# A new list scheduler for the mixers of a three-block transformer kernel, with new filler matmuls

## The chip, the cores and the metric

The kernel runs on one core of a Trainium2 chip. The metric is the device time of one launch in microseconds (us), median of three runs. Lower is better.

## What is computed

The input is 256 tokens of width 1024, float32. Three blocks are applied in turn. Each is: half a SwiGLU feed-forward (width 2816), a mixer, half a second feed-forward, all with residual sums and RMS norms. The first block ends with a final norm, and so does the last.

```python
x = x + 0.5 * swiglu(rms_norm(x, ffn1_norm), w_gate, w_up, w_down)
x = x + hybrid_mixer(rms_norm(x, mix_norm), ...)      # block 1
x = x + 0.5 * swiglu(rms_norm(x, ffn2_norm), ...)
```

The mixer of block 1 (stage 1, "mix1") adds two gated branches: a dilated attention over 4 heads in 3 groups, and RWKV-7, a recurrence per head over 16 heads, `S_t = S_(t-1) diag(w_t) + (S_(t-1) a_t) b_t^T + v_t k_t^T`, `y_t = S_t r_t`, with small decay, rate and gate networks ahead of it and a group norm behind it. The mixer of blocks 2 and 3 (stages 5 and 8, "mix2") has three attentions: a chunked one with a bias by distance (6 heads, kind a), one over keys that an index picks (5 heads, kind b), and one with a latent key and value (5 heads, kind c), and an output product.

## The kernel before, in words

Every product of float32 data with a weight is made of three matmuls (`mm3`, L1584 to L1586): data and weights are split into a high and a low part, and high x high, high x low and low x high are summed in one PSUM bank. Weights stream from HBM in chunks of up to 128 x 2048 numbers (1 MB) into three raw buffers. ScalarE (ACT) copies a chunk's high part (L2130) and VectorE (DVE) subtracts it for the low part (L2493). This is step `split`. The two buffers `whi`/`wlo` alternate.

The order of the whole program is made by the class `Order` before any instruction is written. It appends steps such as `("r_x", s, g, k)` to one list, `P.steps`. Each engine's program then walks this list (`run`) and writes its own part of each step. So all engines meet the steps in the same order, an engine takes its instructions one after the other, and only semaphores tie the engines together.

Stages run one after the other: 0 feed-forward, 1 mix1, 2 feed-forward, 3 norm, 4 feed-forward, 5 mix2, 6 and 7 feed-forward, 8 mix2, 9 feed-forward, 10 norm. Inside a mixer, `woven(steady, rest, *chains)` mixes Python generators. The steady one, `dense`, gives the weight products: `shift_mm` (streams k, v, r of RWKV, 256 columns), `proj` (gates, 512 columns), `up`, `wout`. The other chains give the small steps. The weaver keeps a clock for each engine, fed with the durations of the table `PACE`, and takes the first chain whose input is ready at PE's clock. After each dense step dense rests `rest` us.

RWKV has 8 groups g of two heads. Before, each group is one chain: `r_lora` (decay and rate), `r_tanh`, `r_norm`, `r_scan`, `r_nrm`, `r_exp`, `r_key`, `r_wide`, three `r_scaled`, `r_vb`, `r_ka`, `r_bonus`, `r_pairs`, `r_masks`, `r_dt`, `r_dm0`, `r_g0`; then five rounds k of `r_xz` (POOL clears a buffer), `r_x` (PE, 16 matmuls of 64x32, L1866), `r_xc` (DVE, L2820), `r_d` (PE, 32 matmuls, L1878 and L1885), `r_dd` (DVE, L2830 and L2835); then `r_w`, `r_rp`, `r_yp`, three rounds of `r_st` (DVE, L2855) and `r_s` (PE, L1942 and L1944), `r_ys`, `r_mean`, `r_sq`, `r_var`, `r_wide2`, `r_lg` with `r_turn2`, `r_fin`. At most two groups are in the front part and three in all, by the number of buffers (`Slots`).

`BLANKS` says where PE gets filler matmuls: `('up', 1, 0, 0, 0): 22` puts 22 matmuls of 256 columns on a constant (`still`, L1593) into a free bank ahead of that step. They compute nothing that is used. They come in PE's order like any matmul.

Of the kernel before, what the change touches and what calls it, by code (L numbers as in the profile page):

```python
# [94 lines left out]
def down_after(m):  # L95
# [10 lines left out]
    "split": (("act", 0.6), ("dve", 0.7)), "shift_mm": (("pe", 1.45),), "shift_copy": (("act", 0.6),),  # L106
    "shift_mix": (("dve", 1.5),), "r_lora": (("pe", 0.9),), "r_tanh": (("act", 1.7),), "r_norm": (("pe", 0.45),),
    "r_scan": (("dve", 0.45),), "r_exp": (("act", 1.3),), "r_nrm": (("dve", 0.2),), "r_key": (("dve", 0.9),),
    "r_wide": (("pe", 0.25),), "r_scaled": (("dve", 1.0),), "r_vb": (("pe", 0.45), ("act", 0.8)),
    "r_ka": (("pe", 0.45), ("act", 0.8)), "r_bonus": (("pe", 0.45), ("dve", 0.4)), "r_pairs": (("pe", 1.3),),  # L110
    "r_masks": (("dve", 1.4),), "r_dt": (("dve", 1.0),), "r_dm0": (("pe", 0.35), ("act", 0.4)), "r_g0": (("pe", 0.35), ("act", 0.4)),
    "r_x": (("pe", 0.35),), "r_xc": (("dve", 0.3),), "r_d": (("pe", 0.8),), "r_dd": (("dve", 0.6),),
    "r_w": (("pe", 0.6), ("act", 0.6)), "r_rp": (("pe", 0.6), ("dve", 0.95)), "r_yp": (("pe", 1.1),),
    "r_st": (("dve", 0.25),), "r_s": (("pe", 0.25),), "r_ys": (("act", 0.6),), "r_mean": (("pe", 0.45), ("dve", 0.4)),
    "r_sq": (("act", 0.4),), "r_var": (("pe", 0.45), ("dve", 0.2)), "r_wide2": (("dve", 0.4),), "r_lg": (("pe", 0.9),),
    "rope1": (("dve", 2.2),), "att_qk": (("pe", 0.5), ("act", 0.8)), "att_score": (("pe", 0.9), ("dve", 1.1)),
    "att_soft": (("dve", 0.2), ("act", 1.0)), "att_turn": (("pe", 0.4), ("act", 0.6)),
    "att_out": (("pe", 1.0), ("dve", 0.5)), "up": (("pe", 1.4),), "r_turn2": (("pe", 0.25),), "r_fin": (("dve", 1.3), ("act", 0.4), ("dve", 0.4)), "wout": (("pe", 1.4),),
    "turn_iq": (("pe", 0.45), ("act", 0.6)), "turn_ik": (("pe", 0.15), ("act", 0.4)), "ix_score": (("pe", 0.4), ("act", 0.55)),
    "ix_sum": (("pe", 2.5), ("act", 0.35)), "lat_turn": (("pe", 0.25), ("act", 0.9), ("dve", 0.5)),  # L120
    "latent_up": (("pe", 1.0), ("act", 0.45)), "turn_c": (("pe", 0.35), ("act", 0.6)), "u_score_c": (("pe", 0.25), ("dve", 0.4)),
    "u_score_b": (("pe", 0.6), ("dve", 0.4)), "u_score_a": (("pe", 0.6), ("dve", 0.4)), "u_soft": (("act", 0.45),),
    "u_turn": (("pe", 0.2), ("act", 0.35)), "u_out": (("pe", 0.35),), "turn_b": (("pe", 0.45), ("act", 0.6)),
    "turn_a": (("pe", 0.45), ("act", 0.6)), "turn_out": (("pe", 0.25), ("act", 0.4), ("dve", 0.4)), "wout2": (("pe", 1.4),),
    "in2_out": (("act", 0.6),), "lat_sq": (("act", 1.9),), "lat_scale": (("dve", 0.75), ("act", 1.1)), "bias8": (("act", 1.5),),
    "ix_rope": (("dve", 2.8),), "ix_diag": (("dve", 1.2),), "ix_top": (("dve", 1.5),), "krope": (("dve", 1.2),),
    "ix_mask": (("dve", 0.7),), "brope": (("dve", 1.9),), "qrope": (("dve", 1.4),), "u_norm": (("dve", 0.7),),
    "proj": (("pe", 0.7),), "proj_out": (("dve", 0.7), ("act", 0.6)),
}
HOP = 0.25  # L130

BLANKS = {
    ('turn_x', 1, 0, 0): 6, ('proj', 1, 'qkv', 1, 0): 5, ('proj', 1, 'gate', 0, 0): 14,
    ('proj', 1, 'gate', 0, 4): 2, ('att_turn', 1, 0, 1, 0): 4, ('att_out', 1, 0, 0): 4, ('up', 1, 0, 0, 0): 22,
    ('r_wide', 1, 0): 3, ('r_wide', 1, 1): 3, ('shift_mm', 1, ('k', 1), 0, 4): 6, ('r_bonus', 1, 0): 10,
    ('r_d', 1, 0, 2): 18, ('r_d', 1, 2, 4): 12, ('r_x', 1, 3, 5): 5, ('r_dm0', 1, 4): 4, ('r_d', 1, 4, 4): 7,
    ('r_d', 1, 4, 5): 1, ('r_s', 1, 4, 2): 8, ('r_mean', 1, 4): 2, ('r_var', 1, 4): 2, ('r_s', 1, 5, 1): 3,
    ('r_d', 1, 6, 3): 4, ('r_x', 1, 6, 4): 4, ('r_mean', 1, 6): 5, ('r_d', 1, 7, 5): 2, ('r_rp', 1, 7): 4,  # L140
    ('r_s', 1, 7, 2): 3, ('r_mean', 1, 7): 5, ('r_var', 1, 7): 10, ('r_turn2', 1, 7): 8, ('wout', 1, 3, 1, 0): 22,
    ('turn_merged', 1, 4, 0): 3, ('wo', 1, 3, 0, 0): 6, ('wo', 1, 3, 1, 0): 2, ('proj', 4, 'gh', 0, 0): 27,
    ('turn_x', 5, 0, 0): 6, ('latent_up', 5, 'uq', 0, 0): 6, ('turn_x', 8, 0, 0): 6, ('u_turn', 8, 'a', 0, 0): 2,
    ('latent_up', 8, 'uq', 0, 0): 6,
}
# [182 lines left out]
class Slots:  # L328

    def __init__(self, idx):
        self.free = [(i, None) for i in idx]
        self.at = {}
# [5 lines left out]
    def give(self, key):  # L339
        self.free.append((self.at[key][0], key))  # L340
# [2960 lines left out]
```

## Time and profile before

| what | value |
|---|---|
| median of 3 runs | 1917.9 us (1911.91 to 1919.15) |
| profiled execution, its own time | 1917.34 us |
| its span, first to last instruction | 1915.5 us |
| mean granted TensorE clock | 0.988 |
| PE busy | 1860.2 us (97%) |
| DVE busy | 1202.0 us (63%) |
| ACT busy | 1010.1 us (53%) |
| POOL busy | 91.2 us (5%) |

The span is cut by stage. RWKV runs from about 330 to 635 us, the two mix2 stages from 1044 to 1200 us and from 1560 to 1734 us (the last with the head of the next feed-forward). PE busy is the union of the matmul records. A record of a small matmul is over 0.2 us long though the next starts much earlier, so "busy" covers short waits too.

### The profile page before, as it was taken

The page shows a single profiled execution, that of the slowest core. Times are in us where ns is not written, and L with a number is a line of the kernel's source. Part 1 is how long each engine was busy: PE and PEld are TensorE (multiplying, and loading weights), DVE is VectorE, ACT ScalarE, POOL GpSimd, SP SyncE. Part 2 cuts the span into 40 slices and gives each one's busy share as a digit, 9 for nine tenths or more (in the row PEclk, how much of TensorE's full clock was granted, in tenths as well). Part 3 has the DMA queues.
Part 4 walks back from the last instruction along what each step waited for, and adds up shares of the span by engine and source line. Part 5 has one row for each costly group of instructions (what it writes and reads, how often), then busy time and mean ns, then how long its engine had stood idle before and what let it go on. Part 6 is the DMA issues. An engine that isn't in the chain of part 4 may idle for free.

```text
span 1915.5 us, 31122 instructions
## 1 busy us (share of the span) xinstructions
PE 1860.2 (97%) x12716; PEld 1574.9 (82%) x12716; DVE 1202.0 (63%) x2481; ACT 1010.1 (53%) x2070; POOL 91.2 (5%) x187
## 2 busy tenths in 40 slices
PE   9999999989878999999999999999999999999998
PEld 7888889877766888888888887888888888878887
DVE  5576555666664565766675765657566757666565
ACT  5555555323422355645565666556555656665554
POOL 0000000112210000010000000000000000000000
PEclk9999999899989999999999999999999999999999
DMA  6555443122112345634563343556445633435553
GB/s 239 198 222 206 166 145 110 68 74 76 65 51 95 111 165 198 247 127 158 193 256 109 129 149 110 176 184 235 153 156 195 251 113 129 149 111 187 179 189 115
DMA packets 42718, 296.30 MB, mean 155 GB/s; under 512 B 4832, under 2 KB 4960, under 8 KB 10576
## 3 DMA queue, kind: packets, MB, share of 16 engines
q1 hardware_dynamic: 41184, 288.48, 42.6%
q0 software_dynamic: 1392, 5.83, 0.9%
q8 instruction: 100, 1.64, 0.4%
q14 instruction: 42, 0.34, 0.1%
HBM read 293.25 MB, written 1.05 MB: 154 GB/s over the span
## 4 chain that ended last, share of the span: by engine, by line
PE 90%; DVE 5%; ACT 2%; issue 2%; POOL 1%; DMA 0%; POOLq 0%; DVEq 0%; ACTq 0%
PE PS L1642 21%; PE PS L1584 16%; PE PS L1586 15%; PE PS L1585 15%; PE PS L1644 11%; PE PS L1593 1%; PE PS L2087 1%; DVE wlo L2493 1%; PE PS L1619 1%; PE PS L1885 1%; PE PS L1999 1%; PE PS L1866 1%; PE PS L2076 1%; PE PS L2043 1%; PE PS L2051 1%
## 5 line engine op out<-in xcount | busy, mean ns | idle before, releaser
L2493 DVE TENSOR_TENSOR wlo<-raw,whi 128x512 fp32r<-128x512 f32 (+5 forms) x784 | 614.2, 827 | 195.8 <-ACT whi L2130 189.7
L1642 PE MATMUL PS<-xhl,whi 128*128 128x512 f32 x1728 | 612.8, 398 | 0.0
L2130 ACT ACTIVATE whi<-raw 128x512 fp32r<-128x512 f32 (+5 forms) x784 | 533.3, 735 | 150.7 <-PE PS L1586 148.6
L1644 PE MATMUL PS<-xhl,wlo 128*128 128x256 f32 x1728 | 484.7, 280 | 0.0
L1642 PEld LDWEIGHTS PS<-xhl,whi 128*128 128x128 f32 x1728 | 324.6, 188 | 79.1
L1644 PEld LDWEIGHTS PS<-xhl,wlo 128*128 128x128 f32 x1728 | 326.2, 189 | 2.1
L1584 PE MATMUL PS<-whi,yh 128*128 128x512 f32 (+2 forms) x572 | 227.2, 397 | 3.5 <-DVE yl L2894 3.5
L1586 PE MATMUL PS<-whi,yl 128*128 128x512 f32 (+2 forms) x572 | 223.3, 390 | 0.0
L1585 PE MATMUL PS<-wlo,yh 128*128 128x512 f32 (+2 forms) x572 | 223.2, 390 | 0.0
L2578 DVE TENSOR_TENSOR arena<-arena,PS 128x256 f32<-128x256 f32 x216 | 90.3, 418 | 159.1 <-ACT arena L2200 159.1
L1584 PE MATMUL PS<-whi,xhl 128*128 128x512 f32 (+4 forms) x480 | 189.5, 395 | 0.5 <-DVE wlo L2493 0.4
L1586 PE MATMUL PS<-whi,xhl 128*128 128x512 f32 (+4 forms) x480 | 179.9, 375 | 0.0
L1585 PE MATMUL PS<-wlo,xhl 128*128 128x512 f32 (+4 forms) x480 | 179.3, 374 | 0.0
L1584 PEld LDWEIGHTS PS<-whi,yh 128*128 128x128 f32 x572 | 108.0, 189 | 29.7 <-issue 6.1
L1586 PEld LDWEIGHTS PS<-whi,yl 128*128 128x128 f32 x572 | 108.2, 189 | 23.5
L1585 PEld LDWEIGHTS PS<-wlo,yh 128*128 128x128 f32 x572 | 108.3, 189 | 19.3
L2197 ACT ACTIVATE arena<-arena 128x256 f32<-128x256 f32 x108 | 45.1, 418 | 124.8 <-DVE arena L2578 124.8
L1584 PEld LDWEIGHTS PS<-whi,xhl 128*128 128x128 f32 x480 | 90.3, 188 | 17.3 <-DVE wlo L2493 2.7
L1586 PEld LDWEIGHTS PS<-whi,xhl 128*128 128x128 f32 x480 | 90.1, 188 | 14.1
L1585 PEld LDWEIGHTS PS<-wlo,xhl 128*128 128x128 f32 x480 | 90.5, 189 | 11.3
L2203 ACT ACTIVATE yh<-arena 128x256 fp32r<-128x256 f32 x108 | 45.2, 418 | 102.3 <-DVE arena L2582 102.3
L2586 DVE TENSOR_TENSOR yl<-arena,yh 128x256 fp32r<-128x256 f32 x108 | 45.9, 425 | 52.3 <-ACT yh L2203 52.3
(269 smaller groups left out, 2406.8 us busy)
## 6 DMA issues: line engine op xcount, KB each, us to landing
raw<-wall SPq DMA_DIRECT2D x249, 1024.0 KB, 4.9
raw<-wall SPq DMA_DIRECT2D x12, 768.0 KB, 4.3
raw<-wall SPq DMA_DIRECT2D x8, 968.0 KB, 4.8
raw<-wall SPq DMA_DIRECT2D x4, 896.0 KB, 4.5
arena<-ebias POOLq DMA_DIRECT2D x2, 768.0 KB, 4.8
raw<-wall SPq DMA_DIRECT2D x2, 720.0 KB, 4.1
raw<-wall SPq DMA_DIRECT2D x2, 640.0 KB, 4.4
X<-x SPq DMA_DIRECT2D x2, 512.0 KB, 5.4
```

Source lines behind the costliest of these rows:

```text
L1584: e.matmul(o, wa, xa, start=first, stop=False)
L1585: e.matmul(o, wa, xb, start=False, stop=False)
L1586: return e.matmul(o, wb, xa, start=False, stop=last)
L1593: e.matmul(PS[:, i, 0:256], still[:, 0:128], still[:, :], start=True, stop=True)
L1642: e.matmul(b, hi[:, c0:c0 + 128], xhl[:, k, :, :].rearrange("p a t -> p (a t)"), start=(k == 0), stop=False, skip_group_check=True)
L1644: p = e.matmul(b[:, 0:256], lo[:, c0:c0 + 128], xh[:, k, :], start=False, stop=(k == 7), skip_group_check=True)
L2130: e.activation(whi[slot_of(i)][:, c].bitcast(F32R), raw[i % 3][:, c], copy).then_inc(*M.sig("whi", ("split", i, q)))
L2197: e.activation(g, g, ACT.Silu).then_inc(*M.sig("act", ("silu", s, m)))
L2203: e.activation(hbuf(m)[0], g, copy).then_inc(*M.sig("act", ("hh", s, m)))
L2493: e.tensor_tensor(wlo[slot_of(i)][:, c], raw[i % 3][:, c], whi[slot_of(i)][:, c].bitcast(F32), ALU.subtract).then_inc(*M.sig("wlo", *[("ha ...
L2578: e.tensor_tensor(o, o, bank(("gu", s, m, n))[:, 0:256], ALU.add).then_inc(*M.sig("dve", (key, s, m), ("free", ("gu", s, m, n))))
L2586: e.tensor_tensor(hl, g, hh.bitcast(F32), ALU.subtract).then_inc(*M.sig("dve", ("hl", s, m)))
```

## The change

- The durations in `PACE` are new, several by size of the step (`BY_ROWS`), and POOL gets a clock of its own. The pause between engines (`HOP`) is 0.3 us behind PE, 0.1 behind ACT and DVE, 0.15 behind POOL, instead of 0.25 everywhere. Steps of 64-row matmuls (`QUARTERS`) cost 0.1 us more when PE changes to or from them.
- The weaver keeps times for all that a chain waits for: another chain's step (`after`), a bank (`room`), a buffer (`place`), the split of a weight chunk (`cut_piece`). PE's clock is the main one; work of the other engines is put into the first hole of their plan that holds it (`slip`).
- Each RWKV group is four chains instead of one: `group` (the long one), `decay` (`r_lora`, `r_tanh`, `r_scan`, `r_exp`), `rows` (`r_vb`, `r_ka`, `r_bonus`, `r_g0`), and `gates` (`r_lg`). `r_tanh` gives its square to a step `r_square`, `r_fin` gives its last two to `r_yh` and `r_yl`. `r_xz` for k=1 and 2 is issued ahead of `r_wide`, the others two rounds early.
- Dense rests 1.0 us in RWKV instead of 3.0; in mix2 0.6, 0.3 and 0.5 instead of 0.5, 1 and 9.
- `BLANKS` has 77 entries with 666 matmuls instead of 40 with 272. RWKV's own steps (`r_...`, `shift_mm`) have 400 instead of 129, mix1's others 116 instead of 90, stage 0 has 4 instead of 0, stage 4 has 20 instead of 27, mix2 has 63 and 63 instead of 12 and 14.
- `run` still writes every engine's part in the order of the one list (`line` returns it as it is). A mark, which says when a buffer may be reused, is set behind the last step that touches the buffer (`belongs`), not behind all steps issued so far.

The core of the diff (new entries of `PACE`, the old `BLANKS`, context lines and the reading of marks in mix2 are left out):

```diff
-HOP = 0.25
...
+QUARTERS = {"r_lora", "att_score", "r_pairs", "r_dm0", "r_g0", "r_x", "r_d", "r_w", "r_rp", "r_yp", "r_s", "ix_score",
+            "u_score_a", "u_score_b"}
+FRONT = {"r_lora", "r_square", "r_tanh", "r_norm", "r_scan", "r_exp", "r_nrm", "r_key", "r_wide", "r_scaled", "r_vb",
+         "r_ka", "r_bonus", "r_pairs"}
+HOP = {"pe": 0.3, "act": 0.1, "dve": 0.1, "pool": 0.15}
+LOAD = 4.9
+REST = 1.0
...
+    ('proj', 0, 'gh', 0, 4): 4, ('turn_x', 1, 0, 0): 4, ('proj', 1, 'qkv', 1, 0): 4, ('proj', 1, 'gate', 0, 0): 13,
+    ('att_qk', 1, 0): 15, ('att_out', 1, 0, 0): 8, ('att_turn', 1, 1, 1, 0): 7, ('att_out', 1, 2, 0): 8,
+    ('att_out', 1, 3, 0): 9, ('up', 1, 0, 0, 0): 20, ('r_vb', 1, 0): 5, ('r_vb', 1, 1): 15, ('r_g0', 1, 1): 5,
+    ('r_x', 1, 1, 2): 7, ('r_vb', 1, 2): 7, ('r_lora', 1, 3): 10, ('r_g0', 1, 2): 5, ('r_d', 1, 1, 5): 9,
+    ('r_s', 1, 0, 1): 12, ('r_s', 1, 1, 1): 12, ('r_pairs', 1, 3): 13, ('r_d', 1, 2, 3): 3, ('r_turn2', 1, 1): 16,
+    ('r_norm', 1, 4): 8, ('r_norm', 1, 5): 14, ('r_lora', 1, 5): 10, ('r_x', 1, 3, 4): 5, ('r_var', 1, 2): 6,
+    ('r_d', 1, 3, 4): 4, ('r_g0', 1, 4): 10, ('r_w', 1, 3): 8, ('r_x', 1, 4, 2): 9, ('r_vb', 1, 5): 8,
+    ('r_pairs', 1, 5): 4, ('r_s', 1, 3, 3): 6, ('r_x', 1, 4, 4): 5, ('r_x', 1, 4, 5): 12, ('r_norm', 1, 7): 6,
+    ('r_d', 1, 5, 1): 6, ('r_x', 1, 5, 2): 9, ('r_wide', 1, 6): 16, ('r_s', 1, 4, 2): 10, ('r_vb', 1, 6): 6,
+    ('r_x', 1, 5, 3): 7, ('r_mean', 1, 4): 11, ('r_d', 1, 5, 3): 11, ('r_g0', 1, 6): 6, ('r_dm0', 1, 6): 13,
+    ('r_x', 1, 6, 5): 5, ('r_x', 1, 7, 2): 9, ('r_x', 1, 7, 3): 28, ('r_s', 1, 7, 1): 4, ('r_s', 1, 7, 2): 4,
+    ('r_s', 1, 7, 3): 4, ('r_mean', 1, 7): 4, ('r_var', 1, 7): 8, ('r_turn2', 1, 7): 5, ('wout', 1, 3, 1, 0): 19,
+    ('wo', 1, 1, 0, 1): 6, ('wo', 1, 3, 0, 0): 3, ('proj', 4, 'gh', 0, 0): 20, ('turn_x', 5, 0, 0): 4,
+    ('turn_iq', 5): 4, ('proj', 5, 'in2', 4, 6): 10, ('lat_turn', 5, 0, 0): 4, ('u_out', 5, 'c', 0, 0): 4,
+    ('u_out', 5, 'c', 1, 1): 4, ('u_turn', 5, 'b', 4, 1): 14, ('wout2', 5, 1, 0, 1): 19, ('turn_x', 8, 0, 0): 4,
+    ('turn_iq', 8): 4, ('proj', 8, 'in2', 4, 6): 10, ('lat_turn', 8, 0, 0): 4, ('u_out', 8, 'c', 0, 0): 4,
+    ('u_out', 8, 'c', 1, 1): 4, ('u_turn', 8, 'b', 4, 1): 14, ('wout2', 8, 1, 0, 1): 19,
...
     def take(self, key):
         assert self.free, key
-        self.at[key] = self.free.pop(0)
+        self.hand(key, min(self.free, key=lambda f: self.since.get(f[0], 0.0)))
     def give(self, key):
         self.free.append((self.at[key][0], key))
+        self.since[self.at[key][0]] = self.clock.ready
...
+    def slip(self, eng, ready, us):
+        taken, at = self.taken[eng], max(ready, self.floor)
+        while taken and taken[0][1] < self.now - 60:
+            taken.pop(0)
+        for n, (a, b) in enumerate(taken):
+            if at + us <= a:
+                taken.insert(n, (at, at + us))
+                return at
+            at = max(at, b)
+        taken.append((at, at + us))
+        return at
...
+        return said
     def do(self, *step):
         if step[:5] in self.blanks and self.bank.free:
-            self.steps.append(("fill", self.blanks.pop(step[:5])) + self.bank.free[0])
+            self.steps.append(("fill", self.blanks.pop(step[:5])) + min(
+                self.bank.free, key=lambda f: self.bank.since.get(f[0], 0.0)))
+        n = len(self.steps)
         self.steps.append(step)
-        ready = self.ready
-        for eng, us in PACE.get(step[0], ()):
-            self.now[eng] = max(self.now[eng], ready) + us
-            ready = self.now[eng] + HOP
-        if step[0] != "split":
-            self.ready = ready
+        if step[0] == "split":
+            self.begun[n] = self.cut_piece(step)
+            return
+        ready, read = self.ready, self.weights_of(step)
+        if step[0] in ("shift_copy", "gate_attn", "resid", "proj_out", "in2_out"):
+            ready += HOP["pe"]
+        if read:
+            ready = max(ready, self.cut.get(read[0], (0.0, 0.0))[0 if read[1] else 1])
+        said = {}
+        for eng, us, *aside in self.pace(step):
+            if eng == "pe":
+                quarters = step[0] in QUARTERS
+                said[eng] = max(self.now, ready)
+                self.now = said[eng] + us + 0.1 * (quarters != self.mode)
+                self.mode, end = quarters, self.now
+            else:
+                said[eng] = self.slip(eng, ready, us)
+                end = said[eng] + us
+            self.last_end = end + HOP[eng]
+            if not aside:
+                ready = self.last_end
+        self.begun[n] = said
+        self.ready = self.now if read and step[0] != "latent_up" else ready
+        self.end_of[n] = max(ready, self.last_end) if said else ready
+        if read:
+            self.use_end[read[0]] = ready
...
+    def after(self, *keys):
+        while not all(k in self.did_at for k in keys):
+            yield 1
+        late = max([self.did_at[k] for k in keys], default=0.0)
+        if late > self.ready:
+            self.ready = late
+            yield 2
...
+    def line(self, eng):
+        return range(len(self.steps))
...
+        def decay(g):
+            yield from self.after(("open", g))
             yield from self.room(2)
             for i in range(2):
...
             yield 1
+            self.do("r_scan", s, g)
+            self.did_at["kp0", g] = self.last_end
+            yield 1
+            self.do("r_exp", s, g)
+            self.did("exp", g)
+            yield 1
...
+        def rows(g):
+            G = g // 2
+            yield from self.after(("bt", g), ("exp", g), ("v", G))
+            one("r_vb", g)
+            free("r_vb", g)
+            self.did("vb", g)
+            yield 1
+            yield from self.after(("A", g))
+            one("r_ka", g)
+            free("r_ka", g)
+            self.did("ka", g)
+            yield 1
+            yield from self.after(("rk", g))
+            one("r_bonus", g)
+            free("r_bonus", g)
+            yield 1
+            yield from self.after(("T", g))
+            self.mark("front", g)
+            self.ready = max(self.ready, self.did_at["mark", "front", g])
+            fronts.give(g)
+            yield 1
+            yield from self.room_for_two()
+            pair("r_g0", g)
+            self.did("g0", g)
...
+        def group(g):
+            G = g // 2
+            yield from place(fronts, g)
+            yield from self.after(("k", G))
+            self.did("open", g)
+            self.do("r_square", s, g)
+            yield 1
+            yield from self.room(1)
+            one("r_norm", g)
+            yield 1
+            self.do("r_nrm", s, g)
+            free("r_norm", g)
+            yield 1
+            yield from self.after(("kp0", g))
+            self.do("r_key", s, g)
+            yield 1
+            yield from place(wholes, g)
+            for k in (1, 2):
+                self.do("r_xz", s, g, k)
+            yield from self.after(("exp", g))
+            yield from self.room(1)
+            one("r_wide", g)
+            yield 1
+            self.do("r_scaled", s, g, 0)
+            free("r_wide", g)
+            self.did("bt", g)
...
                 self.do("r_d", s, g, k)
+                if k < 4:
+                    self.do("r_xz", s, g, k + 2)
...
-        self.woven(dense(), 3.0, *(group(g) for g in range(8)))
+        def gates(g):
+            yield from self.after(("lg_in", g))
+            yield from self.room(1)
+            one("r_lg", g)
+            self.did("lg", g)
+            yield 1
+        self.woven(dense(), REST, *[c(g) for g in range(8) for c in (group, decay, rows, gates)])
...
-            self.rest = 9
+            self.rest = 0.5
...
-        self.woven(products(), .5, outs(), index(), latent(), sparse(), near(), *units)
+        self.woven(products(), .6, outs(), index(), latent(), sparse(), near(), *units)
...
         def run(eng, table):
-            for name, *a in P.steps:
-                if name == "mark":
-                    if eng != "sp":
-                        M.mark(eng, ("mark",) + tuple(a))
-                elif name in table:
-                    table[name](*a)
+            line = P.line(eng)
+            place, marks = {n: at for at, n in enumerate(line)}, {}
+            for n, step in enumerate(P.steps):
+                if step[0] == "mark" and eng != "sp":
+                    last = max([place[i] for i in range(n) if P.steps[i][0] in table and belongs(step[1:], P.steps[i])],
+                               default=-1)
+                    marks.setdefault(last, []).append(step)
+            for at, n in enumerate([None] + list(line), -1):
+                if n is not None and P.steps[n][0] in table:
+                    table[P.steps[n][0]](*P.steps[n][1:])
+                for step in marks.get(at, ()):
+                    M.mark(eng, step)
...
-            def r_tanh(s, g):
+            def r_square(s, g):
                 F_ = FR[slot("front", g)]
                 k3 = KZV[g // 2 % 2]["k"][:, g % 2, :]
                 for t in due(*front_free(g), ("dve", ("mix", ("k", g // 2))), COLS):
                     e.wait_ge(*t)
                 e.activation(F_.sq, k3, ACT.Square, scale=col("kk", g)).then_inc(*M.sig("act", ("sq", g)))
-                for t in due(("pe", ("lora", g)), ("dve", ("halves",))):
+            def r_tanh(s, g):
+                F_ = FR[slot("front", g)]
+                for t in due(*front_free(g), ("pe", ("lora", g)), ("dve", ("halves",))):
...
-            def r_fin(s, g):
+            def r_yh(s, g):
...
+            def r_yl(s, g):
+                W_ = WH[slot("whole", g)]
```

## Rows read from the trace of the kernel before

**Rows 1.** Page: busy time of each engine and its share of the span.

```profile
PE 1860.2 (97%) x12716; PEld 1574.9 (82%) x12716; DVE 1202.0 (63%) x2481; ACT 1010.1 (53%) x2070; POOL 91.2 (5%) x187
```

**Rows 2.** Windows: start:end, length, busy PE PEld DVE ACT POOL, clock, DMA share, GB/s.

```profile
197.50:340.00 142.50, 141.92 (x873) 123.05 (x871) 79.32 (x192) 77.70 (x172) 11.83 (x20) 1.00 0.40 141
340.00:635.00 295.00, 259.51 (x4179) 216.81 (x4179) 174.93 (x466) 91.98 (x228) 44.29 (x70) 0.93 0.21 73
...
1044.00:1200.00 156.00, 152.94 (x867) 129.93 (x866) 102.73 (x320) 99.77 (x243) 6.98 (x22) 1.00 0.36 119
1560.00:1734.00 174.00, 170.94 (x955) 144.91 (x954) 112.30 (x343) 110.49 (x269) 7.95 (x25) 1.00 0.34 117
```

**Rows 3.** Groups of instructions from 340 to 635 us, PE.

```profile
L1584 PE MATMUL PS<-xhl,whi 128*128 128x256 f32 x140 | 45.4, 324 | 0.0
...
L1593 PE MATMUL PS<-still 128*128 128x256 f32 x141 | 23.8, 312 | 3.5 <-DVE arena L2820 2.0 <-ACT arena L2293 1.1 <-DVE arena L2835 0.4
...
L1584 PE MATMUL PS<-whi,xhl 128*128 128x512 f32 x32 | 14.3, 447 | 0.0
L1584 PE MATMUL PS<-whi,yh 128*128 128x512 f32 x29 | 14.2, 490 | 3.5 <-DVE yl L2894 3.5
```

**Rows 4.** Waits of PE from 340 to 650 us: total us, times, longest.

```profile
PE PS L1942 <- DVE arena L2855: 5.5, 4, 4.4
PE PS L1866 <- DVE arena L2830: 3.9, 3, 1.4
```

**Rows 5.** Timeline, 546 to 576 us: start, us, engine, line.

```profile
554.62 1.28 DVE L2791 TENSOR_TENSOR arena<-PS,C 128x512 f32<-128x512 f32 x2
555.82 0.47 DVE L2753 SCALAR_TENSOR_TENSOR arena<-arena,C,PS 128x256 f32<-128x256 f32 x1
...
557.13 0.28 DVE L2855 TENSOR_SCALAR arena<-PS,arena 128x64 f32<-128x64 f32 x1
...
557.46 0.49 PE L1942 MATMUL PS<-arena 64*64 64x64 f32 x4 [4.42 <-DVE arena L2855]
```

**Rows 6.** Chain that ended last, 360 to 372 us.

```profile
363.70 0.68 DVE arena L2725
...
364.57 0.72 POOL arena L3100
...
366.16 1.31 POOL arena L3107
...
367.47 1.15 POOL arena L3100
368.62 0.99 POOL arena L3107
369.61 0.28 POOL arena L3112
```

**Rows 7.** Waits of all engines from 340 to 650 us.

```profile
DVE arena L2820 <- POOL arena L3112: 8.5, 4, 3.0
```

**Rows 8.** Timeline of PE around three fillers.

```profile
325.82 2.87 PE L1593 MATMUL PS<-still 128*128 128x256 f32 x22
328.71 0.47 PE L1584 MATMUL PS<-whi,yh 128*128 128x512 f32 x1
329.02 0.39 PE L1585 MATMUL PS<-wlo,yh 128*128 128x512 f32 x1
...
370.33 4.21 PE L1593 MATMUL PS<-still 128*128 128x256 f32 x18 [1.96 <-DVE arena L2820]
...
1106.49 0.96 PE L1593 MATMUL PS<-still 128*128 128x256 f32 x6
1107.29 0.38 PE L1584 MATMUL PS<-whi,yh 128*128 128x480 f32 x1
```

**Rows 9.** Waits of PE from 1044 to 1200 us.

```profile
PE PS L1584 <- DVE early L2493: 1.3, 1, 1.3
PE PS L1619 <- ACT GATE L2148: 0.7, 1, 0.7
```

More of the change, by code:

```diff
@@ L111 @@
[L111 to L115, printed above, removed]
@@ L1018, in group @@
             yield 1
+            yield from self.room(1)
+            one("r_turn2", g)
             yield 1
-            yield from self.room(2)
-            self.bank.take(("r_turn2", g))
-            one("r_lg")
-            self.do("r_turn2", s, g)
+            yield from self.after(("lg", g))
+            self.do("r_fin", s, g)
+            free("r_turn2", g)
+            free("r_lg", g)
             yield 1
-            self.do("r_fin", s, g)
-            self.bank.give(("r_turn2", g))
-            free("r_lg")
+            self.do("r_yh", s, g)
+            yield 1
+            self.do("r_yl", s, g)
             out.add(g)
+            self.did("out", g)
             self.mark("whole", g)
@@ L1054, in unit @@
             S = self.slots["N" if kind == "a" else "S", s]
-            while kind not in made or kind == "b" and "mask" not in made or not (S.free and st.free):
+            yield from self.after((s, kind), *[(s, "mask")] * (kind == "b"))
+            while not (S.free and st.free):
                 yield 1
@@ L1070, in unit @@
             yield 1
-            while kind == "a" and 6 not in made:
-                yield 1
+            yield from self.after(*[(s, 6)] * (kind == "a"))
             if h == 0:
@@ L1084, in unit @@
                 yield 1
-                heads.add((kind, tt))
+                self.did(s, "heads", kind, tt)
             yield 1
@@ L1113, in index @@
                 yield 1
-            made.add("mask")
+            self.did(s, "mask")
         def latent():
-            while 1 not in made:
-                yield 1
+            yield from self.after((s, 1))
             self.do("lat_sq", s)
@@ L1132, in latent @@
             self.turn(("lt", s, 1, 0), "lat_turn", s, 1, 0)
-            made.add("lat")
-            while "ukv" not in made:
-                yield 1
+            self.did(s, "lat")
+            yield from self.after((s, "ukv"))
             for tt in range(2):
@@ L1138, in latent @@
                 yield 1
-            while ("sum", 1) not in made:
-                yield 1
+            yield from self.after((s, ("sum", 1)))
             for j in range(5):
@@ L1156, in sparse @@
                     yield 1
-            while not {("a", 0), ("a", 1)} <= heads:
-                yield 1
+            yield from self.after(*[(s, "heads", "a", tt) for tt in range(2)])
             self.mark("near", s)
@@ L1181, in products @@
                 if j == 5:
[L1182 to L1184 removed]
+                    self.rest = 0.3
+            yield from self.after((s, "lat"))
             for nm, cws in (("uq", (480,)), ("ukv", (320, 320))):
@@ L1214, in products @@
                 yield 1
-            while "out b1" not in made:
-                yield 1
+            yield from self.after((s, "out b1"))
             for n, _ in enumerate(self.tail_row(s, "wout2", "wout2", js, ids, 1)):
@@ L1224, in outs @@
             for kind, ks, tts in (("a", (0,), (0, 1)), ("c", (6,), (0, 1)), ("b0", (2, 4), (0,)), ("b1", (2, 4), (1,))):
-                while not {(kind[0], tt) for tt in tts} <= heads:
-                    yield 1
+                yield from self.after((s, 2), (s, 3), *[(s, "heads", kind[0], tt) for tt in tts])
                 if kind == "c":
```

356 lines of the change are left out of this document (210 added, 146 removed).

## Prediction

> **What bounds the kernel now.** I read the page first. TensorE (PE) is busy 97% of the span and no other engine over 63% [rows 1], so only what shortens PE's own list, or the holes in it, can gain. The windows by stage come next, because an average hides where the holes are. In the attention part of mix1 (197.5 to 340 us) PE misses 0.6 us of 142.5. In RWKV (340 to 635 us) it misses 35.5 us of 295, and the granted clock is 0.93. In the two mix2 stretches it misses 3.1 us each [rows 2]. The reader should see that the change works in three places and that only one has room by this view.
>
 At this level a filler of 18 took from 370.33 to about 374.5 us, 0.23 us each, where 22 at the full level took 2.89 us (325.82 to 328.71), 0.13 each [rows 8].
>
> The waits of PE in RWKV are mostly short. The longest is 4.42 us in one piece, on `r_s` for `r_st` [rows 4]. The timeline shows its cause: `r_st` (L2855) needs 0.28 us, but on DVE it stood behind two `r_masks` (1.28 us together) and the `r_scaled` of another group, because that is where the list put it. PE then waited with its own list behind `r_s` [rows 5]. The second kind is in the chain near 364 us. POOL works off L3100 (0.72), L3107 (1.31), L3100 (1.15), L3107 (0.99) and the clearing L3112 (0.28) one after the other, for two groups, before DVE and then PE go on [rows 6]. DVE waits for this clearing 8.5 us in all, in four places [rows 7]. Both are faults of the order, which the old durations did not see.
>
> **The change, part by part.** The useful work does not change: the same matmuls, copies and DMAs. Three things do: how much waiting is left, how many fillers PE runs, and how long the clock is low.
>
> Price of a filler: 0.13 us at the full clock (2.89 / 22; 6 took 0.80 us, 1106.49 to 1107.29, the same) [rows 8]. All 666 cost 87 us and the old 272 cost 35 us, so PE's list gets 51 us longer. A filler costs nothing where PE would have waited that long anyway, and its full 0.13 us where it would not.
>
> *RWKV before.* 295 us hold 35.5 us without PE and 141 fillers [rows 2, 3], 141 x 0.13 = 18 us. The 41 us at low clock cost less than half of themselves, 20.5 us, since part of them is waiting and fillers already counted; I take 10. That leaves 231 us. This is an upper bound for the work, since a record of a 64-row matmul outlasts the time to the next and so hides short waits.
>
> The lower bound goes by what the steps need. In the table of the change a group's PE parts sum to 11.2 us (of which `r_x` and `r_d` 5 x (0.25 + 0.48)), x 8 = 89. Dense: 140 triples of 256 columns, 32 and 29 triples of 512 [rows 3]. A matmul of 512 columns starts 0.23 us before the next [rows 8], so a triple costs 0.69, and I take 0.36 for the half width: 50 + 22 + 20 = 92. For changes between 64-row and full matmuls, up to 0.1 x 40 x 8 = 32. Sum 213. So the work is between 213 and 231 us; I take 218, near the lower end, because the hidden waits must be somewhere and the table agrees with the rows I can check.
>
> *RWKV after.* Fillers of `r_...` steps 400 and of `wout` 19: 419 x 0.13 = 54.5 us. Each stands where the new plan says PE would wait. The least entry is 3, so waits below some 0.4 us stay bare, and the plan will miss some. Before, 35.5 us were bare; I take 7 now, and 1 for low clock. 218 + 54.5 + 7 + 1 = 280.5 against 295: **14.5 us less**. With the work at 231 and bare waits of 15 it is 301, 6 us more. With work at 213 and waits of 3 it is 271, 24 us less.
>
> What makes less waiting plausible: `r_nrm` (POOL, about 1 us) no longer stands behind L3100 of the same group, so two of the four steps of the chain at 364 us leave the group's start; `r_xz` comes two rounds early, which covers the 8.5 us; `r_lg` with its DMA and `r_vb`, `r_ka` are off the long chain; and the weaver knows when a bank or buffer comes free. What is late next is the five rounds of `r_x`, `r_xc`, `r_d`, `r_dd`, a fixed alternation of PE and DVE. The fillers inside them say so themselves: 28 before `r_x` of group 7, round 3.
>
> *Attention of mix1.* Its steps have 88 fillers instead of 57, 31 more. PE misses only 0.6 us there [rows 2], so the view gives them no cover: 0 if the new order makes the gaps, 4 us if not. I take +1.5.
>
> *mix2, twice.* 51 and 49 more fillers, 6.6 and 6.4 us. Cover is the 3.1 us of holes, of which 1.3 us waits for split weights and 0.7 us for the norm [rows 9], and short hidden waits. Dense no longer rests 9 us near the end, so `wout2` work that covered the last heads of kind b is used earlier, and 33 fillers stand there now. I take +1 each, between -2 and +5. Stages 0 and 4 change by 4 - 7 fillers, under 0.5 us.
>
> *POOL, SP, ACT.* Chunks are loaded in the same order, and no window of mixers has over 0.40 of DMA time [rows 2], so I charge nothing; if a split came late it would cost what it cost in mix2, 1.3 us [rows 9]. `r_square` alone on ACT and two steps for the end of `r_fin` are no new instructions. ACT and DVE have 203 and 120 us free in RWKV [rows 2], which is cover for them, except where order matters, as below.
>
> Sum: -14.5 + 1.5 + 1 + 1 = -11. From the profiled execution, 1917.34 (0.6 us under the median 1917.9, its span 1915.5 and 1.8 around it), this is 1906.3; I say **1906**.
>
> **The rivals.**
> *A, the one order stops DVE (slower).* The new plan puts DVE's work into holes of its calendar (`slip`), also ahead of steps that were listed earlier. The program does not: `line` gives every engine the plain list. A DVE step listed behind another whose PE part comes later waits for it. Rows show the size: 4.42 us of PE for a 0.28 us instruction [rows 4, 5]. Then gaps are not where the fillers are, and a filler runs while the next operand is ready. If half of RWKV's 54.5 us of fillers find no gap, 27 us are added to the 280.5: 308, 13 us more, with the mix2 and attention terms 1934. It decides from about 15 us of misplaced fillers on. Against it: chains are listed roughly as they become ready, so most inversions are under a microsecond.
> The Trainium skill says the same in "TensorE: Matmul & The Clock Gate", under "Architectural detail: the array is 16x 32x32, not 1x 128x128": ScalarE and VectorE queues are strictly first in, first out. By that rule the plan's holes are not to be had, and the time is A's; the trace agrees for DVE, with 4.42 us.
>
> *B, nothing to measure.* Waits become fillers one for one. For: 35.5 + 18 + 10 us of waiting, fillers and slow clock before (63.5) against 54.5 + bare waits after. With work at 226, bare waits 10 and clock 1, RWKV takes 291.5, 3.5 us less, which the other stages give back: 1917.
>
> *C, much better.* Work at 213, bare waits 3, mix2 2 us less each: 1917.3 - 24 + 0 - 4 = 1889. For: RWKV's work is a good quarter below its length. Against: the plan itself holds 54.5 us of gaps.
>
> *D, fillers find no cover at all.* All 51 us on top, with the waits as they are: 1965, less the 10 us of low clock, 1955. Against: PE has 35.5 us of holes in RWKV alone.
>
> **How the numbers follow.** Forecast 0.39 (1897 to 1908), C 0.08, B 0.27 (1909 to 1925), A 0.21, D 0.05. A measurement here tells 0.5% from no change, 9.6 us, so faster means below 1908.3 and slower above 1927.5. Forecast and C are faster, less 0.02 for the forecast's edge: 0.45. B and that edge give 0.29, A and D 0.26. The range leaves out D, the outer part of A and half of C: 1887 to 1936.
>
> **What would show it.** Right: in RWKV PE's bare idle below 15 us, granted clock 0.99 or more, L1593 with some 400 records there, and the stretch from the end of attention to the last `wout` 10 to 20 us shorter; POOL's clearing no longer in DVE's waits; mix2 within 2 us of 156. Wrong by A: PE waits of over 1 us on DVE lines (L2855, L2820, L2830) right behind or ahead of fillers, and DVE steps whose operand was ready long before. Wrong by B: busy time up by the fillers, the stretch as long as before. The prediction falls if work in RWKV is really near 231 us, or if the new places do not meet the gaps.

## The result

The changed kernel takes 1946.29 us (median of 4 runs, 1941.07 to 1947.52) against 1916.41 before. The ratio is 1.0153, 95% interval 1.0125 to 1.0181: 1.5% slower, where I had forecast 0.6% faster. The profiled execution has a span of 1944.0 us, 28.5 more than before.

The page of the kernel after, busy time of each engine, answers to [rows 1]:

```profile
PE 1902.0 (98%) x13094; PEld 1616.7 (83%) x13094; DVE 1198.8 (62%) x2485; ACT 1014.0 (52%) x2074; POOL 89.6 (5%) x187
```

PE is busy 41.8 us longer, and the other engines do what they did. The mean granted clock rose from 0.988 to 0.995. So PE's visible holes shrank, the clock rose, and the kernel still got slower.

Where: I cut both traces at marks that exist in both. A mixer runs from the last gate/up matmul of the feed-forward ahead of it (before: L1642, after: L1852) to the first of the next one; mix1 is also cut at the first `up` matmul. Windows of after, with the columns of [rows 2]: attention of mix1, RWKV with the output products, both mix2.

```profile
189.60:336.40 146.80, 145.90 (x893) 126.63 (x891) 76.47 (x187) 75.55 (x164) 7.66 (x15) 1.00 0.41 144
336.40:698.70 362.30, 342.76 (x4740) 290.97 (x4741) 210.58 (x541) 128.76 (x306) 51.03 (x85) 0.99 0.23 79
...
1039.70:1238.60 198.90, 194.85 (x1069) 164.72 (x1068) 119.42 (x357) 117.12 (x283) 7.73 (x25) 0.99 0.34 113
1577.60:1775.10 197.50, 193.38 (x1070) 163.32 (x1068) 119.55 (x357) 117.16 (x283) 8.31 (x26) 1.00 0.35 117
```

The same cuts of the kernel before:

```profile
187.20:328.70 141.50, 141.37 (x861) 122.93 (x860) 76.41 (x186) 73.71 (x162) 7.30 (x15) 1.00 0.41 146
328.70:689.70 361.00, 323.73 (x4491) 268.73 (x4491) 215.13 (x542) 128.08 (x308) 52.46 (x85) 0.94 0.23 80
...
1031.00:1219.30 188.30, 185.06 (x1019) 156.24 (x1017) 118.86 (x355) 116.57 (x281) 7.98 (x25) 1.00 0.36 120
1558.20:1746.80 188.60, 185.37 (x1021) 156.55 (x1019) 118.89 (x355) 116.57 (x281) 8.57 (x26) 1.00 0.35 122
```

| stretch | before | after | difference |
|---|---|---|---|
| start to the first gate/up matmul | 36.3 | 38.6 | +2.3 |
| attention of mix1 | 141.5 | 146.8 | +5.3 |
| RWKV and output products of mix1 | 361.0 | 362.3 | +1.3 |
| mix2, first | 188.3 | 198.9 | +10.6 |
| mix2, second | 188.6 | 197.5 | +8.9 |

The rest is equal within 0.3 us. The reader should see two things. In the long RWKV stretch PE's missing time fell from 37.3 to 19.5 us and the clock rose from 0.94 to 0.99, and its length did not change. And the two mix2 stages, where before PE missed 3.2 us each, lost 19.5 us together.

What became of the holes is shown by the waits of PE in the same stretch of after (332 to 660 us), which answer to [rows 4] (the two largest sums):

```profile
PE PS L1803 <- DVE arena L3033: 3.0, 3, 1.5
PE PS L1803 <- DVE arena L3048: 2.4, 3, 1.2
```

L1803 is the filler. The longest waits are now the fillers' own: a filler writes into a free bank, and must wait for the last reader of that bank on DVE (L3033 is `r_xc`, L3048 the second half of `r_dd`). In [rows 3] they waited 3.5 us in all, now 8.3 us between 332 and 646.5 us. There are also three times as many of them: 0.025 us of wait per filler before, 0.020 after.

```profile
L1803 PE MATMUL PS<-still 128*128 128x256 f32 x419 | 64.0, 300 | 8.3 <-DVE arena L3033 3.0 <-DVE arena L3048 2.4 <-DVE arena L3043 1.5
```

### The profile page after: what moved, and what is told of

Its sections match the earlier page's. It is cut to its first block, busy times and chain, and to the rows that moved or that the text cites. A ratio compares the mean times of both kernels' runs of the same rounds, so it can differ in the third digit from the quotient of the medians.

```text
span 1944.0 us, 31839 instructions
## 1 busy us (share of the span) xinstructions
PE 1902.0 (98%) x13094; PEld 1616.7 (83%) x13094; DVE 1198.8 (62%) x2485; ACT 1014.0 (52%) x2074; POOL 89.6 (5%) x187
## 4 chain that ended last, share of the span: by engine, by line
PE 88%; DVE 7%; ACT 4%; issue 1%; POOL 1%; DMA 0%; SPq 0%; POOLq 0%; DVEq 0%; ACTq 0%
PE PS L1852 21%; PE PS L1794 15%; PE PS L1796 14%; PE PS L1795 14%; PE PS L1854 11%; PE PS L1803 3%; DVE wlo L2706 1%; ACT arena L2665 1%; PE PS L1829 1%; PE PS L2209 1%; PE PS L2095 1%; PE PS L2297 1%; PE PS L1988 1%; PE PS L2076 1%; PE PS L2253 1%
## 5 line engine op out<-in xcount | busy, mean ns | idle before, releaser
L1852 PE MATMUL PS<-xhl,whi 128*128 128x512 f32 x1728 | 613.1, 399 | 0.0
L1852 PEld LDWEIGHTS PS<-xhl,whi 128*128 128x128 f32 x1728 | 324.9, 188 | 78.9
L1795 PEld LDWEIGHTS PS<-wlo,yh 128*128 128x128 f32 x572 | 107.6, 188 | 19.5
L1803 PE MATMUL PS<-still 128*128 128x256 f32 x646 | 97.9, 298 | 14.2 <-ACT arena L2671 3.5
L1803 PEld LDWEIGHTS PS<-still 128*128 128x128 f32 x646 | 86.3, 197 | 19.7 <-ACT arena L2671 4.0
```

The source lines that it names most:

```text
L1795: e.matmul(o, wa, xb, start=False, stop=False)
L1803: e.matmul(PS[:, i, 0:256], still[:, 0:128], still[:, :], start=True, stop=True)
L1852: e.matmul(b, hi[:, c0:c0 + 128], xhl[:, k, :, :].rearrange("p a t -> p (a t)"), start=(k == 0), stop=False, skip_group_check=True)
```

## The experiments

Four questions: are the fillers the loss, is the one order for all engines, is it the difference between the plan and the run, and what is wrong in mix2. "Bare" means `BLANKS = {}`; no filler computes anything used. Times are medians; ratios stand against the kernel before on the same chip, whose median there was 1914.2 to 1916.3 us. A filler without the wait on its bank wasn't tried.

### Fillers, and an order of its own for each engine

```diff
 # after_bare, before_bare
-BLANKS = { ... }
+BLANKS = {}
 # after_own; after_own_bare has both edits
 def line(self, eng):
-    return range(len(self.steps))
+    order = list(range(len(self.steps)))
+    if eng not in ("act", "dve", "pool"):
+        return order
+    for a, b in zip(self.epochs[::2], self.epochs[1::2]):
+        at, keys = 0.0, {}
+        for n in range(a, b):
+            at = self.begun.get(n, {}).get(eng, at)
+            keys[n] = at
+        order[a:b] = sorted(range(a, b), key=lambda n: (keys[n], n))
+    return order
```

`begun` is the start that the planner's calendar gives a step on each engine, and `epochs` are the stretches made by the weaver. The changed kernel records both and uses neither.

**after_bare.** 

> The changed kernel with BLANKS empty: no filler at all (they compute nothing that is used). Theory F (fillers stand where PE had its next operand ready): RWKV (332 to 646.5 us) gets shorter by up to 403 x 0.13 = 52 us less what a lower clock gives back, each mix2 stage by 63 x 0.13 = 8 us to 154, the whole to about 1890 to 1905. Theory G (they stand in real gaps, the order itself is the slow thing): the time stays within 10 us of 1946, PE's bare idle in RWKV rises by some 45 us, and more of the span is at the lower clock.

**before_bare.** 

> The kernel before with BLANKS empty. It shows what its 272 fillers are worth. Theory F: they too cost about what they last, so it gains up to 20 us. Theory G: they keep the clock and stand in gaps, so it is as fast as before or slower by 5 to 20 us, with more low clock in RWKV. Beside the changed kernel without fillers it compares the two orders alone: F expects that one no slower, G expects it 15 to 30 us slower.

**after_own.** 

> The changed kernel, but ACT, DVE and POOL take the steps inside each mixer by their planned start on that engine, as the planner's calendar has them; PE and SP keep the list, fillers as in the changed kernel. Theory A (one order stops an engine behind a step that is not ready): 20 to 40 us faster, below 1925, and the waits and the bare idle of PE in RWKV go down. Rival (the inversions are under a microsecond and cost nothing): within 8 us of 1946.

**after_own_bare.** 

> Both: own orders and no fillers. If fillers cost (F) and order costs (A), this is the fastest of all, 1870 to 1895. If only order costs, it is near the one with own orders and fillers. If neither, about 1946.

| | one list | own orders |
|---|---|---|
| after, with 666 fillers | 1946.3, 1.0153 (1.0125 to 1.0181) | 1919.5, 1.0028 (1.0016 to 1.0041) |
| after, bare | 1954.4, 1.0211 (1.0196 to 1.0226) | 1879.3, 0.9824 (0.9802 to 0.9847) |
| before, bare | 1915.7, 1.0003 (0.9993 to 1.0012) | |

The fillers are not the loss: without them the changed kernel is 8 us slower. Theory F falls for it, and with no filler in either kernel the new list is 39 us slower than the old one (1954.4 against 1915.7). The one order is a loss: without fillers it costs 75 us, with them 27. With own orders the fillers cost 40 us. In the stretch from `up` the bare kernel has PE missing 57.3 us with one list and 19.3 us with own orders, so there are fewer gaps for them to stand in. For the kernel before, fillers are worth nothing either way.

The windows of mix1 from 188 us (last gate/up matmul) to its end show where; first after_bare, then after_own_bare:

```profile
188.40:708.50 520.10, 451.61 (x5135) 375.73 (x5134) 287.17 (x726) 204.18 (x469) 58.78 (x100) 0.92 0.27 95
```

```profile
187.30:643.00 455.70, 427.71 (x5137) 359.00 (x5135) 288.39 (x726) 204.02 (x469) 60.18 (x100) 0.97 0.31 109
```

The same instructions take 64 us less. PE misses 28 us instead of 68, and the clock is 0.97 instead of 0.92. (The profiled execution of after_own_bare is its slowest, 8 us above the median. own_pool_list, below, has the same mix1, 454.9 us, in an execution at its median; the 8 us are in mix2.)

What shrank is shown by the waits between 330 and 640 us. The first two lines are of after_bare, DVE in front of `r_rp` and PE's `r_x` waiting for `r_dd` of the round before; the last two are the same waits in after_own_bare:

```profile
DVE arena L3039 <- PE PS L2099: 22.8, 8, 5.0
PE PS L2058 <- DVE arena L3025: 9.8, 7, 3.5
...
DVE arena L3048 <- PE PS L2108: 5.8, 7, 1.8
PE PS L2067 <- DVE arena L3034: 0.4, 1, 0.4
```

One place shows how. It is the timeline of after_bare, DVE from 602 to 610 us, then PE from 601 to 610:

```profile
604.69 0.23 DVE L3039 TENSOR_TENSOR arena<-PS,C 128x64 f32<-128x64 f32 x1 [2.90 <-PE PS L2099]
...
605.29 1.28 DVE L2688 TENSOR_TENSOR wlo<-raw,whi 128x512 fp32r<-128x512 f32 x2
606.50 0.47 DVE L3077 SCALAR_TENSOR_TENSOR arena<-arena,C,PS 128x256 f32<-128x256 f32 x1
...
607.86 0.28 DVE L3025 TENSOR_TENSOR arena<-arena,PS 128x128 f32<-128x128 f32 x1
```

```profile
601.72 0.62 PE L2070 MATMUL PS<-arena 64*64 64x32 f32 x16
602.11 1.05 PE L2077 MATMUL PS<-arena 64*64 64x32 f32 x16
...
604.22 0.43 PE L2099 MATMUL PS<-arena 64*64 64x64 f32 x4
608.20 0.65 PE L2058 MATMUL PS<-arena 64*64 64x32 f32 x16 [3.55 <-DVE arena L3025]
```

DVE stood idle for 2.90 us in front of L3039 (`r_rp` of one group), which waited for PE. Behind it in the list was L3025 (first half of `r_dd` of another group), whose matmuls (L2070) were over by about 602.3 us, so for 2.3 of the 2.90 us DVE had work that it could have done. After L3039 and the rest of `r_rp` came a weight split (L2688) and `r_fin` (L3077 and the two behind it), 2.6 us together, and only then L3025, 5.5 us after its operand. PE waited 3.55 us for it. Both parts, the idle wait and the steps put ahead, come of the order.

### Which steps and which engines

**own_split** moves only the split steps of ACT and DVE to their planned place. **own_act** gives an own order to ACT alone. **own_pool_list** gives it to ACT and DVE, not to POOL. **own_rwkv** gives it to all three, but only in the RWKV stretch:

```diff
 # own_act, own_pool_list
-    if eng not in ("act", "dve", "pool"):
+    if eng not in ("act",):            # ("act", "dve") in own_pool_list
 # own_rwkv
-    for a, b in zip(self.epochs[::2], self.epochs[1::2]):
+    for a, b in [self.epochs[2:4]]:
 # own_split: splits keep their order (keys never fall), so do all other steps, and the two rows are merged
+    keys[n] = at = min(at, self.begun.get(n, {}).get(eng, at))   # from the end back
```

> Changed kernel, no fillers; on ACT and DVE only the split steps (high and low part of a weight chunk) move to where the planner's calendar has them, all other steps keep the list's order. To be read against the changed kernel without fillers (1954.4) and the same with own orders on ACT, DVE and POOL (1879.3). Theory S (the 75 us are the splits, which the list hands to ACT and DVE up to 25 us later than the plan counts on): below 1900. Rival T (it is the small steps of the RWKV groups passing one another): above 1935. Both in part: between.

> Changed kernel, no fillers; only ACT takes its own planned order, DVE and POOL keep the list. If the list hurts mostly through ACT: below 1900. If through DVE, the engine with the longer queue: above 1930. Theory S gives a middle value, 1915 to 1940, since the low parts stay late on DVE.

> Changed kernel, no fillers, own orders on ACT and DVE, the list on POOL. If POOL's order matters (it clears buffers and takes the powers): 1895 or more. If not: within 6 us of the 1879 with all three.

> Changed kernel, no fillers; ACT, DVE and POOL take their own planned orders in the RWKV stretch only, the attention part and both mix2 stages keep the list. Theory A by stage: RWKV gives nearly all of the 75 us, so 1880 to 1892. Rival (mix2 needs it too): 1895 to 1910.

| bare, changed planner | us | ratio |
|---|---|---|
| one list | 1954.4 | 1.0211 |
| splits moved | 1959.6 | 1.0224 (1.0197 to 1.0251) |
| own order on ACT | 1940.4 | 1.0127 (1.0101 to 1.0154) |
| own order on ACT and DVE | 1881.1 | 0.9815 (0.9800 to 0.9830) |
| own orders on all three, RWKV only | 1892.6 | 0.9874 (0.9851 to 0.9897) |
| own orders on all three | 1879.3 | 0.9824 |

Theory S falls: the splits are the steps furthest from their planned place, and moving them alone gains nothing. POOL's order makes no difference. ACT's gives 14 us, and DVE's together with ACT's the rest, 59 us more. DVE's order alone wasn't tried. Most of it, 62 of 75 us, is RWKV, 0.6 us beyond what I expected of theory A. The profiled executions of own_rwkv and own_pool_list, 17 us apart (their medians 11), show where the rest is: 3 us in the attention part (146.7 and 143.7), 7 in the two mix2 stages (table below), 6 in RWKV itself (316.8 and 311.2 from the first `up`), 2 in the start.

### Plan and run made to agree, still with one list

```diff
     def slip(self, eng, ready, us):
-        (search the first hole of the calendar that holds the step)
+        taken = self.taken[eng]
+        at = max(ready, self.floor, taken[-1][1] if taken else 0.0)
+        taken.append((at, at + us))
         return at
```

> Changed kernel, no fillers, one list for all engines, but the planner's calendar puts a step of ACT, DVE or POOL only behind those already listed on that engine (no holes used), as the engines will really run it. Theory M (the loss is the difference between the plan and the run): the planner now lists what it can keep, below 1925. Rival L (one list costs, whatever the plan knows): within 12 us of the 1954 without fillers.

1919.28 us, ratio 1.0019 (1.0008 to 1.0030): 35 us less than the 1954.4 with holes in the calendar. Theory M holds, for nearly half of the 75 us. PE's order changed with the planner's knowledge; the engines still took one list. The rest, 40 us, is the distance from one list with a plan that fits it to own orders. By stage the gain is all in mix1, 41 us; the two mix2 stages got longer, from 195.7 and 197.3 to 200.1 and 200.2. So there a calendar that fits the run did not give a better list. With the holes closed, the new list is within 4 us of the old one, fillers in neither (1919.3 against 1915.7). The rest of the planner's change (durations, pauses, four chains for one) was not taken apart in mix1. The window of mix1 in it, for comparison with the two above:

```profile
187.80:666.80 479.00, 440.23 (x5135) 366.21 (x5134) 286.13 (x726) 204.22 (x469) 59.37 (x100) 0.94 0.30 104
```

### What is wrong in mix2

```diff
 # after_rest (with fillers), own_rest (own orders, bare)
-                    self.rest = 0.3
+                    self.rest = 1
-            self.rest = 0.5
+            self.rest = 9
-        self.woven(products(), .6, ...)
+        self.woven(products(), .5, ...)
 # mix2_old: old PACE, pause 0.25, old weaver, no times in after() and room(), old choice of banks, in mix2 only
-                yield from self.after((s, 2), (s, 3), *[(s, "heads", kind[0], tt) for tt in tts])
+                yield from self.after(*[(s, "heads", kind[0], tt) for tt in tts])
+        self.woven_plain(products(), .5, ...)
 # mix2_durations: as mix2_old, but new durations and pauses; mix2_newweaver: new weaver and pauses, old durations
```

> Changed kernel with its fillers, but in mix2 dense rests .5, 1 and 9 us as before the change (instead of .6, .3 and .5). Theory R (mix2 lost its cover at the end because the weight products are used up early): each mix2 stage goes from 162 back to 152 to 156, the whole to 1926 to 1936. Rival (the 63 fillers and the new order of the small steps cost it): within 5 us of 1946.

> Own orders on ACT, DVE and POOL, no fillers, and the old rests in mix2. Theory R: some 8 us less than the 1879.3 with the new rests. Rival: 1875 to 1885, the same.

> Own orders in mix1, no fillers, and the two mix2 stages listed by the old weaver with the old durations and rests (nearly step for step the list of before). If the new order of mix2 is what costs it 8 us a stage: both mix2 stages back to 151 to 153 us and the whole at 1862 to 1870. If it were fillers or a neighbour stage, 1879 stays.

> The changed kernel as it is (one list, its fillers in mix1 and the stages around it), only the two mix2 stages are listed by the old weaver with the old durations, and have no fillers. If the mix2 stages' loss is their new list and the rest does not depend on it: both back to the length of before, the whole at 1924 to 1930. Rival (the stages hand their loss on): above 1935.

> As the fastest so far (own orders in mix1, no fillers, old weaver and old rests in mix2, 1870.8), but the old weaver in mix2 works with the new durations and pauses. Theory D (the new durations make the worse list of mix2): the mix2 stages get 5 to 10 us longer each, the whole 1880 to 1892. Rival W (the new weaver, which puts a chain off until its input, bank or split is there by the plan, makes it): within 6 us of 1870.8.

> Own orders in mix1, no fillers, new weaver and new rests in mix2, but there with the old durations per step. Theory D: near the old length of mix2, the whole 1870 to 1880. Rival W: mix2 stays 5 to 10 us longer each, the whole 1885 to 1900.

In all four with mix2 in their names the mix2 stages have one list; own orders, where they have them, are in mix1 alone. In mix2_durations some values of mix2 come out changed and the cause is not known, so its time is weaker evidence than the others.

| kernel | us | ratio | mix2, first and second |
|---|---|---|---|
| before | 1916.4 | | 188.3, 188.6 |
| after | 1946.3 | 1.0153 | 198.9, 197.5 |
| before, bare | 1915.7 | 1.0003 | 188.0, 188.6 |
| after, bare | 1954.4 | 1.0211 | 195.7, 197.3 |
| in-order calendar, bare | 1919.3 | 1.0019 | 200.1, 200.2 |
| after_rest | 1957.3 | 1.0216 (1.0186 to 1.0245) | 204.1, 203.9 |
| own_rest | 1891.3 | 0.9879 (0.9849 to 0.9908) | 198.0, 197.4 |
| own orders, bare | 1879.3 | 0.9824 | 193.1, 199.6 (execution of 1887.4) |
| own orders on ACT and DVE, bare | 1881.1 | 0.9815 | 194.5, 191.7 |
| own orders in RWKV only, bare | 1892.6 | 0.9874 | 197.1, 195.7 |
| mix2_old | 1870.8 | 0.9760 (0.9744 to 0.9776) | 188.4, 188.5 |
| change_mix2_old | 1926.2 | 1.0054 (1.0033 to 1.0075) | 188.3, 188.6 |
| mix2_durations | 1910.5 | 0.9979 (0.9966 to 0.9991) | 205.8, 210.6 |
| mix2_newweaver | 1919.2 | 1.0024 (1.0006 to 1.0043) | 212.4, 212.2 |

Windows of the two mix2 stages of change_mix2_old:

```profile
1040.40:1228.70 188.30, 184.39 (x1007) 154.59 (x1005) 118.87 (x355) 116.94 (x281) 7.97 (x25) 1.00 0.35 120
1567.50:1756.10 188.60, 183.96 (x1007) 154.73 (x1005) 118.87 (x355) 116.56 (x281) 8.57 (x26) 1.00 0.35 122
```

With the old list mix2 has its old length to 0.1 us, and the whole change loses 20.1 of its 29.9 us. So the losses of the stages add up. In mix2 it is the new list, not its fillers (bare it is 195.7 and 197.3), not the rests (restored, it is 5 to 6 us worse), and only in part the one order (bare against bare the two stages lose 16 us together, and own orders on ACT and DVE take some 7 of them back). after_rest and own_rest, 1957.3 and 1891.3 us, are both slower than theory R and its rival allowed; mix2_old is 0.8 us above the range expected of it, and change_mix2_old inside. Which part of the planner makes the loss is not settled: the old weaver with the new durations and the new weaver with the old durations are both worse than either pair that belongs together, and 18 us or more above what I had expected of them. Theory D falls as sole cause by mix2_newweaver; rival W falls only by mix2_durations, the weaker evidence. What mix2_old restores besides, the choice of banks and the condition of `outs`, was not tried by itself.

mix2_old is also the fastest version: 1870.8 us, 2.4% under the kernel before and 3.9% under the changed one. Its mix1 takes 453.3 us.

## Why the prediction was wrong

**What bounds the kernel.** PE, as said. But I read the room for change only from PE's holes, and by that view mix2 had none. It had room to lose.

**Price of a filler.** About 0.13 us holds where it runs free (in the kernel after, the 4 in stage 0 take 0.57 us, 17.09 to 17.66). I left out that a filler is itself a waiting instruction: it waits for its bank, 8.3 us in RWKV. Whether the next step would have waited as long without it, no run shows.

**RWKV after, the step that failed.** I had 14.5 us less; measured it is 1.3 us more up to the next feed-forward. The table sets the terms of my sum, made for 340 to 635 us, beside the measured ones. The last two columns are for the longer stretch of the result's table, from the first `up` to the next feed-forward, so the changes are to be compared and not the levels; fillers are priced at 0.13 us and low clock at a quarter of its time, as in the prediction, and "work" is what is left over, so these two columns add up by construction. (The forecast's 14.5 came from 295 less 280.5; its terms as rounded give 14.)

| term, change in us | forecast | after | after_own |
|---|---|---|---|
| PE's bare idle | 35.5 to 7: -28.5 | 37.3 to 19.5: -17.8 | 37.3 to 8.7: -28.6 |
| work with its hidden waits | 231 to 218: -13 | 293.2 to 287.3: -5.9 | 293.2 to 280.5: -12.7 |
| low clock | 10 to 1: -9 | 10 to 2.5: -7.5 | 10 to 0: -10 |
| fillers | 18 to 54.5: +36.5 | 20.5 to 53: +32.5 | 20.5 to 53: +32.5 |
| sum | -14 | +1.3 | -18.8 |

Two terms were mis-sized: the bare idle, which I left at 7 us and which is 19.5, and the work with its hidden waits, put at 218 between bounds of 213 and 231, from which my sum took 13 us and of which only 6 went. Together the two misses are 18 us. So my signs were met in part only: the records of the filler are there, 419, and POOL's clearing is gone from DVE's waits, but bare idle is above 15 us (17.6 from 332 to 646.5 us, at a clock of 0.98), and the stretch is not shorter. The last column shows why. It is the same kernel with the same fillers, and only ACT, DVE and POOL take their planned orders:

```profile
335.10:677.30 342.20, 333.54 (x4739) 285.87 (x4740) 212.87 (x541) 129.13 (x306) 53.02 (x85) 1.00 0.23 83
```

There both terms come out as I had them. My sum was near for the plan, and I charged it to a program that can't run the plan: the step that failed is taking the planner's waits for those of the run while every engine keeps the one list. "The plan will miss some" stood in the prediction, sized at 7 us.

**Rival A.** It is what the experiments show: DVE and ACT stopped by the one list. It costs 27 us with the fillers (1946.3 against 1919.5), 20 of them in this stretch, and 75 us without, 62 of them in RWKV; 35 of the 75 go with the calendar's holes. I gave it 0.21, and wrote against it that most inversions are under a microsecond. DVE's waits in front of `r_rp`, eight of them and 22.8 us in after_bare, the longest 5.0, are longer, though not all of that time had a ready step behind it. Its price was wrong as well: it gave 1934, 12 us too little, and I had the fillers find no gap. They found one, made by the stopped engines; taking them out does not help. By its length alone the stretch looks like rival B (busy time up by the fillers, length as before); the run with own orders tells the two apart.
By the Trainium skill's rule on strict first in, first out queues for ScalarE and VectorE ("TensorE: Matmul & The Clock Gate", under "Architectural detail: the array is 16x 32x32, not 1x 128x128"), cited in the prediction, the time had to come out as A's, slower, and it did: own_pool_list and the bare changed kernel differ only in the order of these two queues, 1881.1 against 1954.4.

**Sums.** Rival D's 1965 should be 1968 (1917 and 51 us on top), and its 1955 then 1958. No decision hung on it. The 0.23 us of a 512-column matmul does not show in [rows 8], whose two starts are 0.31 us apart; it is in the stage 0 rows of the same trace, 15.55 and 15.78 us.

**Attention.** +1.5 forecast, at most 4; it is +5.3. The bare kernel is no shorter there (146.7 us, against 141.1 of the bare kernel before), so this is the list, too. With the in-order calendar it is 142.8.

**mix2.** +1 each, at most 5; measured +10.6 and +8.9. The sign was right and the bound was not: I priced fillers and the cover for them, and the fillers cost at most 3.2 us of it. In a stage in which PE missed only 3.2 us a new list has little to gain, and how much it can lose the waits of before cannot tell.

**POOL, splits, loads.** As said: POOL's order is worth nothing (own_pool_list), DVE no longer waits for its clearing, and moving the splits alone gains nothing.

**Stage 0.** I had under 0.5 us, and it is +2.3 to the first gate/up matmul. The added filler ahead of the first `proj` waits 1.54 us for ACT to write the constant `still`. But kernels without any filler, with the same first steps, reach that matmul anywhere between 36.2 and 38.1 us, so the filler's share is not settled.

## What to carry to other kernels

A planner must model the order that the hardware will keep. If its calendar lets a step pass another, the program must let it pass too; here the change, with holes in its calendar and one list for all, cost 30 us, and the same planner with own orders for ACT, DVE and POOL and no fillers gave 35. Place fillers last and against the kernel as it will run: the same 666 were worth 8 us with one order and cost 40 with the other. In a stage that is already full, keep the old order until the new one has beaten it there.

## What the runs showed of the hardware

More fillers and a higher clock did not make a faster kernel. after_own had no low clock in its mixers and took 1919.5 us; after_own_bare had 27.3 us at 1.2 GHz in RWKV alone and took 1879.3. The kernel before has the same time without any of its 272 fillers (ratio 1.0003), though it then spends 54.6 us at 1.2 GHz in the stretch from `up` instead of 41.0.

PE's busy share hides waits. A record of a 64-row matmul lasts 0.19 us or more while 16 of them run in 0.43 us (L2058 in after_bare, 600.80), and the kernel before, with PE busy for 97% of its span, still had 2.4% to give by new orders and by leaving out the fillers (mix2_old).
